# Moving the FFNs' gated tiles by 32 bytes in SBUF in a three-layer fp32 kernel

## The reference

```
def swiglu(x, w_in, w_out):
    a, b = jnp.split(x @ w_in, 2, axis=-1)
    return (jax.nn.silu(a) * b) @ w_out

x = x + 0.5 * swiglu(rms_norm(x, g), w_in, w_out)     # w_in 1024 x 5632, w_out 2816 x 1024
```

## Time and profile before

| what | value |
|---|---|
| median of 3 runs | 1748.65 us (1746.57 to 1749.03) |
| span of the profiled execution | 1746.7 us |
| TensorE matmuls | busy 1732.6 us, 99% of the span |
| VectorE, ScalarE | 61% and 53% |
| granted TensorE clock, mean | 0.997 |
| matmuls with `hT` or `hT_last` stationary | 1584 |

### The profile page before, as it was taken

One profiled execution on the slowest core, in us unless ns is written; L12 is line 12 of the kernel. 1 busy time (PEld: TensorE's weight loads), 2 busy tenths in 40 slices (PEclk: granted clock), 3 DMA queues, 4 the chain that ended last, 5 costly groups with the idle time before them and its releaser, 6 DMA issues.

```text
span 1746.7 us, 31179 instructions
## 1 busy us (share of the span) xinstructions
PE 1732.6 (99%) x12568; PEld 1589.0 (91%) x12568; DVE 1072.8 (61%) x1500; ACT 930.8 (53%) x1269; POOL 34.4 (2%) x60
## 2 busy tenths in 40 slices
PE   9999999999999999999999999999999999999998
PEld 9999888999899999888898999899999888989997
DVE  6555787655665565646686555755574557776555
ACT  6444677444454455576746444644464577664443
POOL 0000220000000000000000000000000000000000
PEclk9999999999999999999999999999999999999999
DMA  8655524655555555553355555655555543446552
GB/s 326 243 192 191 189 104 154 229 188 196 220 210 194 191 192 202 176 201 134 122 193 188 195 192 196 232 208 192 192 205 175 187 169 122 169 157 220 189 194 95
DMA packets 47551, 328.58 MB, mean 188 GB/s; under 512 B 5488, under 2 KB 5744, under 8 KB 9072
## 3 DMA queue, kind: packets, MB, share of 16 engines
q1 hardware_dynamic: 44640, 316.93, 50.5%
q10 hardware_dynamic: 2832, 10.54, 1.7%
HBM read 326.39 MB, written 1.05 MB: 187 GB/s over the span
## 4 chain that ended last, share of the span: by engine, by line
PE 94%; ACT 3%; DVE 1%; issue 1%; DMA 0%; POOL 0%; SPq 0%; DVEq 0%; POOLq 0%; ACTq 0%
PE work L1735 19%; PE work L1737 19%; PE work L1736 19%; PE acc L1737 8%; PE acc L1736 8%; PE acc L1735 8%; PE work L1975 4%; PE work L1844 3%; PE acc L2059 1%; PE acc L2041 1%; ACT prob L853 1%; PE acc L2051 1%; ACT hi L659 1%; DMA xT_raw<-xT 0%; PE work L1798 0%
## 5 line engine op out<-in xcount | busy, mean ns | idle before, releaser
L1157 DVE TENSOR_TENSOR lo<-raw,hi 128x2048 fp32r<-128x2048 f32 x271 | 620.3, 2291 | 321.7 <-ACT hi L659 321.4
L659 ACT ACTIVATE hi<-raw 128x2048 fp32r<-128x2048 f32 x271 | 518.8, 1915 | 376.3 <-PE work L1737 349.6
L1735 PE MATMUL work<-xT_hi,hi 128*128 128x256 f32 x2464 | 687.0, 279 | 3.0 <-ACT merge L843 2.5
L1736 PE MATMUL work<-xT_lo,hi 128*128 128x256 f32 x2464 | 682.5, 277 | 0.0
L1737 PE MATMUL work<-xT_hi,lo 128*128 128x256 f32 x2464 | 682.5, 277 | 0.0
L1735 PEld LDWEIGHTS work<-xT_hi,hi 128*128 128x128 f32 x2464 | 463.9, 188 | 12.4 <-issue 6.9
L1736 PEld LDWEIGHTS work<-xT_lo,hi 128*128 128x128 f32 x2464 | 464.6, 189 | 2.4
L1737 PEld LDWEIGHTS work<-xT_hi,lo 128*128 128x128 f32 x2464 | 464.1, 188 | 0.0
L1737 PE MATMUL acc<-hi,hT_lo 128*128 128x512 f32 x480 | 189.1, 394 | 0.0
L1736 PE MATMUL acc<-lo,hT_hi 128*128 128x512 f32 x480 | 188.2, 392 | 0.0
L1735 PE MATMUL acc<-hi,hT_hi 128*128 128x512 f32 x480 | 186.4, 388 | 0.0
(11 more groups left out here) (323 smaller groups left out, 2092.7 us busy)
## 6 DMA issues: line engine op xcount, KB each, us to landing
raw<-stream SPq DMA_DIRECT2D x297, 1024.0 KB, 4.8
mem_in<-mem ACTq DMA_DIRECT2D x3, 1024.0 KB, 6.1
post<-post ACTq DMA_DIRECT2D x6, 512.0 KB, 4.5
memT_raw<-mem2T ACTq DMA_DIRECT2D x2, 1024.0 KB, 7.5
xT_raw<-xT SPq DMA_DIRECT2D x2, 512.0 KB, 5.7
raw<-stream SPq DMA_DIRECT2D x2, 512.0 KB, 6.9
x<-x SPq DMA_DIRECT2D x2, 512.0 KB, 10.7
memT_raw<-mem1T ACTq DMA_DIRECT2D x1, 1024.0 KB, 10.7
```

The source lines that it names most:

```text
L659: nc.scalar.activation(dst, raw[:, s, :], ACT.Copy).then_inc(hi_ready, 1)
L1157: nc.vector.tensor_tensor(lo[:, s, :], raw[:, s, :], hi[:, s, :].bitcast(F32), ALU.subtract).then_inc(lo_ready, 1)
L1735: nc.tensor.matmul(dst, a_hi, b_hi, start=start, stop=False)
L1736: nc.tensor.matmul(dst, a_hi, b_lo, start=False, stop=False)
```

## The change

The rooms of `qT` and of `probT` grow by 512 bytes each, and four tiles that share those rooms begin 32 bytes later. They go from 64 to 96 modulo 128. Every other tile behind them moves by 512 or 1024 bytes and keeps its place modulo 512. No instruction, wait, loop or order is changed.

```
-        r_qT = room(4096)
+        r_qT = room(4096 + 512)
         qT = place("qT", [P, 4, T], r_qT)
         lru_g = place("lru_g", [P, LRU_TILES, T], r_qT)
-        hT_hi = place("hT_hi", [P, 2, T], r_qT, F32R)
-        hT_lo = place("hT_lo", [P, 2, T], r_qT + 2048, F32R)
+        hT_hi = place("hT_hi", [P, 2, T], r_qT + H_OFF, F32R)
+        hT_lo = place("hT_lo", [P, 2, T], r_qT + H_OFF + 2048, F32R)
...
-        r_pT = room(4096)
+        r_pT = room(4096 + 512)
...
-        hT_last = [place(f"hT_last_{part}", [P, 2, T], r_pT + 2048 * n, F32R) for n, part in enumerate(("hi", "lo"))]
+        hT_last = [place(f"hT_last_{part}", [P, 2, T], r_pT + H_OFF + 2048 * n, F32R) for n, part in enumerate(("hi", "lo"))]
...
 X_AT = 217 * 512 + 320
+H_OFF = 32
```

## The result

| | before | after |
|---|---|---|
| median of 4 runs, us | 1748.84 (1746.57 to 1750.66) | 1775.49 (1774.81 to 1776.86) |
| ratio, with its 95% interval | | 1.0154 (1.0141 to 1.0168) |
| span of the profiled execution, us | 1746.7 | 1773.6 |
| turn from one `chunk_out` to the next, us | 16.40 | 16.91 |

The kernel became 1.5% slower, 26.7 us by the medians. I had forecast 1748.6, with a range up to 1759.0. The prediction was wrong.

The account below looks back on a forecast made before the run. TensorE was taken as the bound, its matmuls busy 1732.6 of 1746.7 us. All four terms were 0, so 1746.7 us profiled, 1.95 us below the median; forecast 1748.6 us, range 1742.5 to 1759.0.

Parts of the forecast that it names:

- The reads of the stationary operand: TensorE's 1584 matmuls with moved stationary tiles: 0 taken, bounds 3.5 us gained to 6.9 us lost.
- The junction: Turn from `chunk_out` to `chunk_in`, 54 times: no change taken, bounds 1.6 us gained to 21.7 us lost.
- Rival B: `chunk_in` behind `chunk_out` holds the slow pace: 0.41 us per junction, all 53 give 1770.4 us; chance 0.26.
- "nearly all" of the junctions: Case where nearly all turns from `chunk_out` to `chunk_in` hold the slow pace: chance 0.06, left out of the range.
- The writes: ScalarE's and VectorE's writes of the moved tiles (L754, L780, L811, L1274, L1298): 0 taken, with 9.35 us of cover.
- the other tiles' move: Tiles moved by 512 or 1024 bytes: 0 taken, both ends inside the other terms' bounds.
- The turn: Sign, one `chunk_out` to the next: 16.40 us if right, 0.11 more for slow `chunk_out`, 0.41 more for a held junction.
- The gap that I had weighed: 512-column matmuls: 228.8 ns in the trace against the skill's 215.8, 13 ns more for fp32r; sum kept at 0.

Follow-up runs that it names:

- the kernels named above: Kernel before with `xT` at 0 or 96 and `hT` at 64 modulo 128: 1801.86, 1794.51 us; `hT_lo` 128 bytes later, `hT_hi` at 96 or 0: 1754.11, 1750.79 us.
- at 0 with 32: Kernel before with `hT_hi` moved to 0 and `hT_lo` to 32 modulo 128: 1778.86 us, ratio 1.0174.
- the other mixtures: Kernel before with `hT_hi`, `hT_lo` at 64, 96 modulo 128: 1749.85 us; at 96, 64: 1754.11 us; at 0, 64: 1750.79 us.

## Why the prediction was wrong

**The reads of the stationary operand.** This step failed: "By all of these the place of the stationary operand costs nothing, so I take 0." I had priced fp32r matmuls by fp32 ones, L2094 and L2041. (At L2041 `memkT` is the moving operand and `qmemT` the stationary one. Both begin at 64 modulo 128, so the places compared were 96 and 64 as I said; the distances were 96 and 0.) The price was my upper bound, 4.5 ns, on nearly all of the matmuls: 24 x 4.5 = 0.11 us a turn, measured 0.10, some 6 us. The prediction named this as a way to fail ("if the pace of fp32r matmuls, unlike that of the fp32 ones, depends on the place"), and two facts stood against the rows that I used. They differ in data type from the matmuls that the change touches. And the trace showed two paces of the fp32r stream at one and the same place, the 2.4 GHz level throughout, so something other than the columns set its pace.

**The junction.** This step failed too: "Its five slow matmuls cost 0.60 - 5 x 0.1133 = 0.03 us over the fast pace; I take no change." All but a few of the junctions hold the slow pace, 0.40 us each, so its upper bound of 21.7 us came true as well. Rival B had what happened, its place and its price, 0.41 us a junction; that the first loads meet the stream otherwise, its reason, was not shown, and that both slow terms come together was in none of its cases. 1748.65 + 21.7 + 6.9 = 1777.3; measured 1775.5. I gave "nearly all" of the junctions 0.06 and left it out of the range. I argued from "53 of 54 junctions leave"; but 50 of them are one case met 50 times, the same instructions at the same places, not 50 trials, and they say nothing of how near that case lies to the edge. The only trials with another start were the four junctions behind two transposes, and one of the four, held.

**What was right.** The writes cost nothing (L754 634 ns, L1274 692), the other tiles' move cost nothing, and weight loads of `hT_hi` kept their 187 to 188 ns. The turn was the right thing to watch, and the added parts that it was to show (0.11 and 0.41) are those it showed.

**The gap that I had weighed.** The Trainium skill (TensorE: Matmul & The Clock Gate, Back-to-back issue gap) puts the gap of a warm matmul at N / 2.4 + 2.5, which gives 109.2 ns for 256 columns and 215.8 for 512. No distance tried brought these fp32r streams to it: the best were 113.3 and 226.7 ns.

**What stays open.** Shown: moving the stationary operand against the moving one changes the pace of `chunk_out` (226.7 ns at 0, 228.9 at 64, 233 at 32 and 96, when it comes from a fast `chunk_in`; at 0 from a slow one too), and at the distance 64 moving both together doesn't. Not shown: that 128 is the period. Modulo 512 the distances were 256 for 0, 288 for 32, 224 for 96, and 192 for 64 (320 in the kernels named above). Nor is it shown that 32 and 96 have a pace of their own: 233 ns is also the slow pace at 64, so the place may only decide which of two paces the stream keeps. Shown: whether `chunk_in` leaves the slow pace isn't decided by the pace of `chunk_out`, and can be turned at one and the same place by where, and with what, `chunk_out` ends. That it is a phase between the loads and the stream was only argued, and what makes the slow pace is open; I have no rule that tells the outcome from the places (24 matmuls: held at 96, at 0 and at 0 with 32; left at 64, at 32 and, but for three turns, at the other mixtures). Nor do the runs tell whether both 256-column halves or only the earlier end of the 512-column run does it.

## What to carry to other kernels

When TensorE is the bound, hold the pace of its stream from starts, stretch by stretch, against the same instruction elsewhere in the trace: a second pace at the same clock means that a small shift may move hundreds of matmuls from one to the other. Count repeats of one loop as one observation, and when a change touches the operands of such a stream keep the range open to the slow pace in all of it. For fp32r products, try the places of the stationary tiles against those of the moving ones in steps of 32 bytes, and, if the stream stays slow behind a junction, another break there, such as one matmul cut in two.

## What the runs showed of the hardware

- The pace of these fp32r matmuls depends on where their operands stand to one another in SBUF: all tiles 32 bytes later give 16.40 us a turn, as before, the stationary gated ones alone 16.91. That was tried at one distance.
- By the distance modulo 128 in the kernels that ran: 256 columns, 113.3 or 117.8 ns at 64, 120.0 at 0, 118.3 at 96; 512 columns, 226.7 ns at 0, 228.9 or 233.3 at 64, 233 at 32 and 96.
- A stream of 256-column fp32r matmuls can keep a slow pace for all of 96 matmuls with no wait, at the 2.4 GHz level, and be freed or held by the break ahead of it: 10.91 against 11.31 us. 512-column ones can do either behind slow ones: the first 24 with `memT`, at distance 64, follow `hT_last` at 228.7 ns in the changed kernel, and at 233.3 ns in the kernel before, where `hT_last` stood at 64 too and was as slow.
